# A decode stage reordered: from groups of four pages to units of one head pair, across batch boundaries

## The chip, the cores and the metric

The kernel runs on 1 core of a Trainium2 chip. The metric is the device time of one execution in microseconds (us), median of the runs. The engines are TensorE (PE, its weight loads apart as PEld), VectorE (DVE), ScalarE (ACT), GpSimd (POOL) and SyncE (SP). Each has its own instruction queue, worked off strictly in order; they meet through semaphores that the kernel waits on and raises by hand.

## The reference, cut to what matters

One inference step of a two-layer decoder trunk: a prompt of 1024 tokens and 8 decode batches of 4 new tokens each. The change touches only the decode attention of layer 0, over a paged cache of 4096 past tokens (32 pages of 128) and 8 heads of 64:

```python
kpast = cache_k[i][page_table].reshape(Bd, P, H_FOX, HEAD_DIM)
vpast = cache_v[i][page_table].reshape(Bd, P, H_FOX, HEAD_DIM)
c = jnp.cumsum(lf_all, axis=1).transpose(0, 2, 1)          # log forget values, past and new
s = jnp.einsum('bqhd,bkhd->bhqk', q, k_all) * FOX_SCALE
s = s + cq[..., :, None] - c[:, :, None, :]
p = softmax(where(kpos <= qpos, s, -inf))
o = jnp.einsum('bhqk,bkhd->bqhd', p, v_all)
```

All is float32. The kernel gets that precision by splitting an operand into a high part (fp32r) and a low part (operand minus high part), and by a matmul for each.

## The kernel before, in words

The blocks run one after the other: norm, retention, prompt attention (fox), **decode** (decode_block), output projection, and the second layer. Only decode_block changes. In it, a batch's keys come in 8 groups of 4 pages and its values in 16 pieces of 2 pages; a page of keys or values is 128 rows of 2 KB (256 KB), fetched by one DMA. What each engine does for one batch:

- SP loads keys, 4 pages a group, into a ring of 4 groups (L1555); it waits until PE has turned the group that was in that place.
- PE transposes keys (turn_keys, L1609: for each of 4 head pairs j, 4 transposes of 128x128 into PSUM bank kt[j]); computes scores (L1622, one matmul for the forget bias per group; L1626 and L1627, one each for the high and low part of each head pair); computes the scores of the new tokens (L1635, L1637); turns the probabilities (L1647, 16 transposes; L1654 for the new ones); multiplies values (L1665 and L1667, two each per piece, thus 4 matmuls a piece; at the end L1672 for the new values).
- ACT makes the high parts: of keys (L1878, one per group and head pair), of values (L1889, one per piece, 128x1024), and of scores (L1893) and probabilities (L1908). It takes the exponentials (L1899, L1901).
- DVE makes the low parts of the keys from PSUM and the high part (L1723), adds up scores (L1751) and their maxima (L1754), finds the maximum of the batch (L1760 to L1771), makes the low parts of probabilities (L1780), and writes up the heads at the end (L1803 to L1815).
- The low parts of values are divided: of pieces with p % 4 == 3 POOL makes both pages (one 128x1024 instruction); of the other 12 pieces, DVE makes the first page (L1732, 128x512) and POOL the second (L1575, 128x512).
- POOL also loads values, 4 pages a group, into a ring of 4 groups (L1566), one group late: after the two pieces of group n it waits for both low parts of group n-1 and then issues the 4 DMAs of group n+3.

High and low parts of values lie in rings of VRING = 4 pieces; a slot is free when PE has used its piece (v_used).

The order of each queue is written out by hand. There are DB + 1 rounds of 8 groups. In round r, group g, every engine does its whole part of the four head pairs of group g of batch r (PE then the scores of group g-1), and then the value pieces of batch r-1 that two tables give: SLOT_PIECES for PE (pieces 0, 1 in group 2; then three a group; 14, 15 in group 7), AHEAD_PIECES for ACT and DVE (pieces 0, 1 in group 1; 13 to 15 in group 6). The last scores of a batch, its maxima, the queries of the next batch and the heads of the batch before stand in DVE's queue between two rounds, ahead of the next round's keys (L1850 to L1856). The last round has values only.

Before the first round, PE, DVE and ACT prepare the forget biases (L1683 to L1698, L1834 to L1848); SP's loads of small tables stand ahead of them. The tile lf holds the page sums for it, and sc the scores; qz and selz are the stationary operands of the scores.

Of the kernel before, what the change touches and what calls it, by code (L numbers as in the profile page):

```python
# [18 lines left out]
F32 = mybir.dt.float32  # L19
# [1393 lines left out]
def both_on_pool(p):  # L1413

    return p % 4 == 3


def on_vector(p):

    return sum(not both_on_pool(q) for q in range(p + 1))  # L1420


def decode_block(nc, e, a):
# [18 lines left out]
    with ExitStack() as ctx:  # L1442
# [8 lines left out]
        lf = sb("lf", [P, DB, H, NPG])  # L1451
# [4 lines left out]
        qz = sb("qz", [P, pairs, ZW], F32R)  # L1456
        selz = sb("selz", [P, ZW], F32R)
# [9 lines left out]
        sc = sb("sc", [2 * rows, PAST // 2])  # L1467
# [45 lines left out]
        v_lo_first = c.begin("v_lo_first_ready", on_vector(VPIECES - 1))  # L1513
        v_lo_last = c.begin("v_lo_last_ready", VPIECES)
# [20 lines left out]
        with nc.Block() as block:  # L1535
# [24 lines left out]
            def _(pool):  # L1560
# [9 lines left out]
                def split_values(r, p):  # L1570

                    first = 0 if both_on_pool(p) else 1
                    at = VP * p % (RING * PG)
                    pool.wait_ge(v_hi_ready.sem, v_hi_ready.at(r, p + 1))
                    pool.tensor_tensor(v_lo[p % VRING][:, first:VP, :], v[:, at + first:at + VP, :],  # L1575
                                       v_hi[p % VRING][:, first:VP, :].bitcast(F32), ALU.subtract).then_inc(
                        v_lo_last.sem, 1)
# [4 lines left out]
                pool.memset(qz[:].bitcast(F32), 0.0)  # L1582
                pool.memset(selz[:].bitcast(F32), 0.0).then_inc(own_ready.sem, 1)
# [6 lines left out]
                for n in range(DB * GROUPS):  # L1590
                    r, g = n // GROUPS, n % GROUPS
                    for p in (2 * g, 2 * g + 1):
                        split_values(r, p)
                    if n > 0 and n - 1 + RING < DB * GROUPS:
                        last = n - 1
                        p = 2 * (last % GROUPS) + 1
                        pool.wait_ge(v_lo_first.sem, v_lo_first.at(last // GROUPS, on_vector(p)))
                        pool.wait_ge(v_lo_last.sem, v_lo_last.at(last // GROUPS, p + 1))
                        load_values(last + RING)

            @block.tensor
            def _(pe):
                def turn_keys(r, g):
                    landed = k_landed[g % RING]
                    pe.wait_ge(landed.sem, landed.at(r, 16 * PG * (g // RING + 1)))
                    for j in range(pairs):
                        pe.wait_ge(kt_read[j].sem, kt_read[j].at(r, g))
                        for i in range(PG):
                            ins = pe.transpose(kt[j][:, PAGE * i:PAGE * i + PAGE],  # L1609
                                               k[g % RING][:, i, P * j:P * j + P], e.ident[:])  # L1610
                        ins.then_inc(kt_written[j].sem, 1)

                def scores(r, g):
                    x, cols = g // 2, window(g)
                    bank = sbk[x % 2]
                    if g % 2 == 0:
                        pe.wait_ge(sb_read[x % 2].sem, sb_read[x % 2].at(r, x // 2))
                    if g == 0:
                        pe.wait_ge(q_ready.sem, q_ready.at(r, 1))
                    if r == 0:  # L1620
                        pe.wait_ge(ct_ready.sem, ct_ready.at(0, g + 1))
                    pe.matmul(bank[:], selz[:, cols], ct[:, BANK * g:BANK * g + BANK], start=(g % 2 == 0), stop=False)  # L1622
                    for j in range(pairs):
                        pe.wait_ge(kt_read[j].sem, kt_read[j].at(r, g + 1))
                        last = g % 2 == 1 and j == pairs - 1
                        pe.matmul(bank[:], qz[:, j, cols], k_hi[g % 2][:, j, :], start=False, stop=False)  # L1626
                        mm = pe.matmul(bank[:], qz[:, j, cols], k_lo[g % 2][:, j, :], start=False, stop=last)  # L1627
                    if g % 2 == 1:
                        mm.then_inc(sb_written[x % 2].sem, 1)
# [26 lines left out]
                def values(r, p):  # L1656
# [3 lines left out]
                    pe.wait_ge(v_lo_first.sem, v_lo_first.at(r, on_vector(p)))  # L1660
                    pe.wait_ge(v_lo_last.sem, v_lo_last.at(r, p + 1))
                    for i in range(VP):
                        n, parity = block_of(VP * p + i)
                        stationary = pt[:, n, parity, :, :].rearrange("p s c -> p (s c)")
                        pe.matmul(outb[0:2 * rows, :], stationary, v_hi[p % VRING][:, i, :],  # L1665
                                  start=(p == 0 and i == 0), stop=False)
                        mm = pe.matmul(outb[0:2 * rows, :], stationary, v_lo[p % VRING][:, i, :], start=False,  # L1667
                                       stop=False)
# [17 lines left out]
                by_page = lf[:].rearrange("p b h g -> p (b h) g")  # L1686
# [13 lines left out]
                for r in range(DB + 1):  # L1700
                    for g in range(GROUPS):
                        if r < DB:
                            turn_keys(r, g)
                            if g > 0:
                                scores(r, g - 1)
                        if r > 0:
                            if g == 1:
                                turn_probabilities(r - 1)
                            if g == 3:
                                turn_new(r - 1)  # L1710
                            for p in SLOT_PIECES.get(g, ()):
                                values(r - 1, p)
                    if r < DB:
                        new_scores(r)
                        scores(r, GROUPS - 1)

            @block.vector
            def _(dve):
                def split_keys(r, g):

                    for j in range(pairs):
                        dve.wait_ge(kt_hi[j].sem, kt_hi[j].at(r, g + 1))
                        dve.tensor_tensor(k_lo[g % 2][:, j, :], kt[j][:], k_hi[g % 2][:, j, :].bitcast(F32),  # L1723
                                          ALU.subtract).then_inc(kt_read[j].sem, 1)

                def split_values(r, p):

                    if both_on_pool(p):
                        return
                    at = VP * p % (RING * PG)  # L1730
                    dve.wait_ge(v_hi_ready.sem, v_hi_ready.at(r, p + 1))
                    dve.tensor_tensor(v_lo[p % VRING][:, 0, :], v[:, at, :], v_hi[p % VRING][:, 0, :].bitcast(F32),  # L1732
                                      ALU.subtract).then_inc(v_lo_first.sem, 1)

                def queries(r):
                    own = e.q_own[:, r, :].rearrange("p (j c) -> p j c", j=pairs)
                    hi = qz[:, :, rows:2 * rows]
                    dve.tensor_copy(hi, own).then_inc(steps_q.sem, 1)
                    dve.tensor_copy(selz[:, rows:2 * rows], pick[:, r, :])
                    dve.wait_ge(steps_q.sem, steps_q.at(r, 1))  # L1740
                    dve.tensor_tensor(qz[:, :, 3 * rows:4 * rows], own, hi.bitcast(F32), ALU.subtract).then_inc(
# [107 lines left out]
                for r in range(DB + 1):  # L1849
                    if r > 0:  # L1850
                        store_scores(r - 1, GROUPS // 2 - 1)
                        maxes(r - 1)
                        if r < DB:
                            queries(r)
                    if r > 1:
                        heads(r - 2)  # L1856
                    for g in range(GROUPS):
                        if r < DB:
                            split_keys(r, g)
                        if r > 0:  # L1860
                            if g == 1:
                                probabilities(r - 1)
                                sums(r - 1)
                            if g == 3:
                                new_probabilities(r - 1)
                            for p in AHEAD_PIECES.get(g, ()):
                                split_values(r - 1, p)
                        if r < DB and g in (2, 4, 6):
                            store_scores(r, g // 2 - 1)
                heads(DB - 1)  # L1870

            @block.scalar
            def _(act):
                def split_keys(r, g):

                    for j in range(pairs):
                        act.wait_ge(kt_written[j].sem, kt_written[j].at(r, g + 1))
                        act.activation(k_hi[g % 2][:, j, :], kt[j][:], ACT.Copy).then_inc(kt_hi[j].sem, 1)  # L1878
# [571 lines left out]
```

## Time and profile before

| what | value |
|---|---|
| median of 3 runs | 2839.48 us (2836.92 to 2842.32) |
| profiled execution, its own time | 2842.4 us |
| its span, first to last instruction | 2840.7 us |
| PE busy in the span | 2465.6 us (87%) |
| DVE, ACT, POOL busy | 1015.6, 895.5, 729.4 us |
| mean granted TensorE clock | 0.925 |
| keys and values moved in decode | 512 DMAs of 256 KB |

The profiled execution's own time is 1.7 us above its span, which lies around the span, and 2.9 us above the median. Busy shares are means over stages with different limits; decode lies from about 1068 to 1697 us of the span, and the rows below are of that stretch. "Clock" is the share of full speed (2.4 GHz) that TensorE was granted. A matmul's duration in the trace overlaps the next one's: the distance between starts is what one costs.

### The profile page before, as it was taken

How to read it: one execution, taken by the hardware profiler on the slowest of the kernel's cores; microseconds unless marked ns; L12 is line 12 of the kernel's file. 1: busy time of each engine (PE TensorE's matmuls, PEld its weight loads, DVE VectorE, ACT ScalarE, POOL GpSimd, SP SyncE). 2: the span in 40 equal slices, each digit the busy share in tenths (PEclk: the TensorE clock that was granted, in tenths of full speed). 3: DMA queues.
4: the chain of work that ended last, by engine and by line, in shares of the span. 5: the costliest groups of instructions: out<-in, count | busy, mean ns of one | idle time of the engine just before them, and what ended most of it. 6: DMA issues, size and time to landing. Idle time of an engine off the chain costs nothing. (4 is left out here: it accounts for less than half of the span.)

```text
span 2840.7 us, 36413 instructions
## 1 busy us (share of the span) xinstructions
PE 2465.6 (87%) x11784; PEld 1969.8 (69%) x11784; DVE 1015.6 (36%) x1532; ACT 895.5 (32%) x1388; POOL 729.4 (26%) x642
## 2 busy tenths in 40 slices
PE   6999999499999797777877747969988999995899
PEld 6999999377667456555555526857776888784787
DVE  3244334512443555766676650030002311131000
ACT  4232232222232223555555422141113223423200
POOL 1211111131010001555555555211112111210611
PEclk8999999699999898999899958979999999998999
DMA  5122110211200007777777525432112211212531
GB/s 131 31 51 64 41 42 24 63 45 30 52 0 23 7 16 246 253 234 235 229 241 237 175 88 166 118 135 93 63 63 95 94 62 62 91 65 82 168 95 59
DMA packets 241975, 289.12 MB, mean 102 GB/s; under 512 B 66954, under 2 KB 169740, under 8 KB 241740
## 3 DMA queue, kind: packets, MB, share of 16 engines
q1 hardware_dynamic: 203548, 185.00, 22.3%
q0 software_dynamic: 20480, 67.13, 6.9%
q10 hardware_dynamic: 17840, 35.69, 3.5%
q8 instruction: 52, 0.85, 0.1%
q14 instruction: 55, 0.45, 0.0%
HBM read 247.47 MB, written 41.32 MB: 102 GB/s over the span
## 5 line engine op out<-in xcount | busy, mean ns | idle before, releaser
L201 PE MATMUL bank<-whi,x_hi 128*128 128x512 f32 (+1 forms) x1728 | 663.6, 384 | 33.1 <-POOL wlo L188 27.4
L205 PE MATMUL bank<-whi,x_lo 128*128 128x512 f32 (+1 forms) x1728 | 655.7, 379 | 0.0
L203 PE MATMUL bank<-wlo,x_hi 128*128 128x512 f32 (+1 forms) x1728 | 654.8, 379 | 0.0
L188 POOL TENSOR_TENSOR wlo<-wraw,whi 128x512 fp32r<-128x512 f32 (+1 forms) x192 | 227.2, 1218 | 853.5 <-ACT whi L181 853.5
L201 PEld LDWEIGHTS bank<-whi,x_hi 128*128 128x128 f32 x1728 | 328.4, 190 | 100.8 <-POOL wlo L188 24.8
L230 ACT ACTIVATE projected<-bank 128x512 f32<-128x512 f32 (+1 forms) x216 | 120.4, 563 | 798.1 <-PE bank L205 777.4
L205 PEld LDWEIGHTS bank<-whi,x_lo 128*128 128x128 f32 x1728 | 328.7, 190 | 52.3
L203 PEld LDWEIGHTS bank<-wlo,x_hi 128*128 128x128 f32 x1728 | 329.7, 191 | 50.1 <-issue 0.4
L1575 POOL TENSOR_TENSOR dec_v_lo<-dec_v,dec_v_hi 128x512 fp32r<-128x512 f32 (+1 forms) x128 | 205.6, 1625 | 230.5 <-ACT dec_v_hi L1889 229.6
L1665 PE MATMUL bank<-dec_v_hi,dec_pt 128*64 128x512 f32 x256 | 111.8, 437 | 89.7 <-POOL dec_v_lo L1575 55.6
L1609 PE MATMUL bank<-ident,dec_k 128*128 128x128 f32 x1024 | 154.7, 315 | 40.3 <-DVE dec_kt_lo L1723 38.4
L1609 PEld LDWEIGHTS bank<-ident,dec_k 128*128 128x128 f32 x1024 | 143.8, 166 | 54.3 <-issue 43.1
L1732 DVE TENSOR_TENSOR dec_v_lo<-dec_v,dec_v_hi 128x512 fp32r<-128x512 f32 x96 | 154.9, 1640 | 58.9 <-ACT dec_v_hi L1889 58.3
L1878 ACT ACTIVATE dec_kt_hi<-bank 128x512 fp32r<-128x512 f32 x256 | 138.0, 602 | 118.7 <-PE bank L1609 117.8
L1723 DVE TENSOR_TENSOR dec_kt_lo<-bank,dec_kt_hi 128x512 fp32r<-128x512 f32 x256 | 163.2, 681 | 33.3 <-ACT dec_kt_hi L1878 32.2
L501 PE MATMUL bank<-out_whi,out_mhi 128*128 128x512 f32 x392 | 154.7, 395 | 12.0 <-POOL out_mlo L482 12.0
L2224 DVE SCALAR_TENSOR_TENSOR gm_m<-bank,gm_bias,gm_ug 128x256 f32<-128x256 f32 x64 | 25.8, 476 | 359.1 <-ACT gm_ug L2252 359.1
L502 PE MATMUL bank<-out_wlo,out_mhi 128*128 128x512 f32 x392 | 154.0, 393 | 0.0
L503 PE MATMUL bank<-out_whi,out_mlo 128*128 128x512 f32 x392 | 153.9, 393 | 0.0
L534 DVE TENSOR_TENSOR out_y<-bank,out_x 128x512 f32<-128x512 f32 (+1 forms) x36 | 24.5, 689 | 346.5 <-PE bank L503 263.9
L1566 POOL DMA_DIRECT2D dec_v<-cache_v x256 | 137.8, 541 | 39.5 <-issue 36.8
L1889 ACT ACTIVATE dec_v_hi<-dec_v 128x1024 fp32r<-128x1024 f32 x128 | 128.7, 1053 | 36.9 <-PE bank L1667 25.6
(279 smaller groups left out, 3396.8 us busy)
## 6 DMA issues: line engine op xcount, KB each, us to landing
dec_v<-cache_v POOLq DMA_DIRECT2D x256, 256.0 KB, 4.0
dec_k<-cache_k SPq DMA_DIRECT2D x256, 256.0 KB, 3.1
wraw<-w_in_even SPq DMA_DIRECT2D x32, 512.0 KB, 5.9
wraw<-w_in_odd SPq DMA_DIRECT2D x16, 1024.0 KB, 8.3
gv<-projected ACTq DMA_DIRECT2D x4, 2304.0 KB, 8.3
gm_v<-gv SPq DMA_DIRECT2D x8, 1152.0 KB, 5.9
m<-gm_mt ACTq DMA_DIRECT2D x8, 1056.0 KB, 4.1
wraw<-w_in_odd SPq DMA_DIRECT2D x4, 2048.0 KB, 8.8
```

The source lines that it names most:

```text
L188: pool.tensor_tensor(e.wlo[:, k, 0:width], e.wraw[:, k, 0:width], e.whi[:, k, 0:width].bitcast(F32), ALU.subtract).then_inc(e.w_ready.sem, 1)
L201: pe.matmul(bank[:, 0:width], e.xhi[:, k, c:c + P], e.whi[:, k, 0:width], start=(k == 0), stop=False)
L203: pe.matmul(bank[:, 0:width], e.xhi[:, k, c:c + P], e.wlo[:, k, 0:width], start=False, stop=False)
L205: mm = pe.matmul(bank[:, 0:width], e.xlo[:, k, c:c + P], e.whi[:, k, 0:width], start=False, stop=(k == KD - 1))
L501: pe.matmul(bank[:], mhi[slot][:, k, :], whi[:, k, cols], start=(k == 0), stop=False)
L502: pe.matmul(bank[:], mhi[slot][:, k, :], wlo[:, k, cols], start=False, stop=False)
L503: mm = pe.matmul(bank[:], mlo[slot][:, k, :], whi[:, k, cols], start=False, stop=(k == kt - 1))
L1575: pool.tensor_tensor(v_lo[p % VRING][:, first:VP, :], v[:, at + first:at + VP, :], v_hi[p % VRING][:, first:VP, :].bitcast(F32), ALU.subtr ...
L1609: ins = pe.transpose(kt[j][:, PAGE * i:PAGE * i + PAGE], k[g % RING][:, i, P * j:P * j + P], e.ident[:])
L1723: dve.tensor_tensor(k_lo[g % 2][:, j, :], kt[j][:], k_hi[g % 2][:, j, :].bitcast(F32), ALU.subtract).then_inc(kt_read[j].sem, 1)
L1732: dve.tensor_tensor(v_lo[p % VRING][:, 0, :], v[:, at, :], v_hi[p % VRING][:, 0, :].bitcast(F32), ALU.subtract).then_inc(v_lo_first.sem, 1)
L1878: act.activation(k_hi[g % 2][:, j, :], kt[j][:], ACT.Copy).then_inc(kt_hi[j].sem, 1)
```

## The change

Decode's order is rewritten in units u of one head pair: 32 units a batch (4 head pairs times 8 groups), running through from batch to batch without a break. In unit u, PE turns the keys of head pair u % 4 of group u / 4 and computes the scores of the same head pair of the group before; ACT and DVE split that head pair. The other work is hung in at fixed units after a batch's first: the sums of scores at 12, 20, 28 and 36 (the last with the maxima), new scores and the next batch's queries at 20, exponentials at 38, probabilities at 42, new probabilities and sums at 43, value piece p on PE at 44 + 3p/2 (thus 44 to 66), on ACT five units earlier and on DVE four units earlier, heads at 68. So batch r's values run beside batch r+1's keys from its unit 12 to its unit 34, that is up to 2 units into batch r+2.

Also:
- The low part of a value piece is made whole, in one 128x1024 instruction: on DVE for p % 3 == 2 (5 of 16 pieces), on POOL for the other 11.
- POOL issues the loads of group n+4 right after the second piece of group n (no longer one group late), and waits ahead of them for DVE's low part where one of the two pieces is DVE's.
- VRING goes from 4 to 5; qz and selz get two buffers each (two more memsets on POOL ahead of the first load); lf and sc share one tile.

The core of the diff (the semaphores and declarations that only follow from it are left out):

```diff
-VRING = 4
+VRING = 5
-SLOT_PIECES = {2: (0, 1), 3: (2, 3, 4), 4: (5, 6, 7), 5: (8, 9, 10), 6: (11, 12, 13), 7: (14, 15)}
-AHEAD_PIECES = {1: (0, 1), 2: (2, 3), 3: (4, 5, 6), 4: (7, 8, 9), 5: (10, 11, 12), 6: (13, 14, 15)}
+SLOTS = H // 2
+UNITS = GROUPS * SLOTS
+NEW_AT, EXP_AT, TURN, FIRST_VALUE, LEAD = 20, UNITS + 6, UNITS + 10, UNITS + 12, 5
+LOW = [2 * SLOTS * x + 3 * SLOTS for x in range(GROUPS // 2)]
+VALUE_AT = [FIRST_VALUE + 3 * p // 2 for p in range(VPIECES)]
+HEADS_AT = VALUE_AT[-1] + 2
 def on_vector(p):
-    return sum(not both_on_pool(q) for q in range(p + 1))
+    return p % 3 == 2
+def rounds_at(u, at):
+    r = (u - at) // UNITS
+    return r if (u - at) % UNITS == 0 and 0 <= r < DB else None
+def pieces_at(u, lead):
+    return [(r, p) for r in range(DB) for p in range(VPIECES) if UNITS * r + VALUE_AT[p] - lead == u]
...
 # POOL
+                for i in range(2):
+                    pool.memset(qz[i][:].bitcast(F32), 0.0)
+                    ins = pool.memset(selz[i][:].bitcast(F32), 0.0)
+                ins.then_inc(own_ready.sem, 1)
...
+                for n in range(DB * VPIECES):
+                    r, p = n // VPIECES, n % VPIECES
+                    if not on_vector(p):
                         split_values(r, p)
+                    following = n // 2 + RING
+                    if p % 2 == 1 and following < DB * GROUPS:
+                        if on_vector(p) or on_vector(p - 1):
+                            pool.wait_ge(v_lo_vector.sem, v_lo_vector.at(r, by_vector(p)))
+                        if not on_vector(p) or not on_vector(p - 1):
+                            pool.wait_ge(v_lo_pool.sem, v_lo_pool.at(r, by_pool(p)))
+                        load_values(following)
...
 # PE
+                for u in range(UNITS * (DB - 1) + HEADS_AT):
+                    n, j = u // SLOTS, u % SLOTS
+                    if n < DB * GROUPS:
+                        turn_keys(n // GROUPS, n % GROUPS, j)
+                    if 0 < n <= DB * GROUPS:
+                        scores((n - 1) // GROUPS, (n - 1) % GROUPS, j)
+                    if rounds_at(u, NEW_AT) is not None:
+                        new_scores(rounds_at(u, NEW_AT))
+                    if rounds_at(u, TURN) is not None:
+                        turn_probabilities(rounds_at(u, TURN))
+                    if rounds_at(u, TURN + 1) is not None:
+                        turn_new(rounds_at(u, TURN + 1))
+                    for r, p in pieces_at(u, 0):
+                        values(r, p)
...
 # DVE
+                for u in range(UNITS * (DB - 1) + HEADS_AT + 3):
+                    n, j = u // SLOTS, u % SLOTS
+                    for x in range(GROUPS // 2):
+                        r = rounds_at(u, LOW[x])
+                        if r is not None:
+                            store_scores(r, x)
+                            if x == GROUPS // 2 - 1:
+                                maxes(r)
+                    if n < DB * GROUPS:
+                        split_keys(n // GROUPS, n % GROUPS, j)
+                    if rounds_at(u, NEW_AT) is not None and rounds_at(u, NEW_AT) + 1 < DB:
+                        queries(rounds_at(u, NEW_AT) + 1)
+                    if rounds_at(u, TURN) is not None:
+                        probabilities(rounds_at(u, TURN))
+                    if rounds_at(u, TURN + 1) is not None:
+                        new_probabilities(rounds_at(u, TURN + 1))
+                        sums(rounds_at(u, TURN + 1))
+                    for r, p in pieces_at(u, LEAD - 1):
+                        if on_vector(p):
+                            split_values(r, p)
+                    if rounds_at(u, HEADS_AT) is not None:
+                        heads(rounds_at(u, HEADS_AT))
...
 # ACT
+                for u in range(UNITS * (DB - 1) + HEADS_AT + 3):
+                    n, j = u // SLOTS, u % SLOTS
+                    for x in range(GROUPS // 2):
+                        if rounds_at(u, LOW[x]) is not None:
+                            low_scores(rounds_at(u, LOW[x]), x)
+                    if n < DB * GROUPS:
+                        split_keys(n // GROUPS, n % GROUPS, j)
+                    if rounds_at(u, EXP_AT) is not None:
+                        exponentials(rounds_at(u, EXP_AT))
+                    if rounds_at(u, TURN) is not None:
+                        probabilities(rounds_at(u, TURN))
+                    for r, p in pieces_at(u, LEAD):
+                        split_values(r, p)
```

## Rows read from the trace of the kernel before

**Rows 1.** Stretches: us; PE, PEld, DVE, ACT, POOL busy (count); clock; DMA share, GB/s.
```profile
1099.00:1132.30 33.30, 33.30 (x211) 29.11 (x212) 25.13 (x40) 19.24 (x36) 0.00 (x0) 0.95 0.66 192
1132.30:1635.50 503.20, 389.67 (x2052) 288.78 (x2050) 348.39 (x521) 271.49 (x421) 294.49 (x332) 0.91 0.70 228
1635.50:1690.00 54.50, 31.77 (x83) 14.05 (x83) 34.84 (x31) 20.34 (x24) 36.67 (x36) 0.59 0.29 97
```
**Rows 2.** Last step of a batch's maximum: ns min/median/max, first and last start.
```profile
L1771 DVE TENSOR_SCALAR dec_neg_max<-dec_top x8: 144/144/144, 1135.4 to 1635.5; 32x1 f32<-32x1 f32 x8
```
**Rows 3.** PE in order of time, batches 0 and 1: start, us, instruction, count.
```profile
1104.27 0.48 PE L1622 MATMUL bank<-dec_ct,dec_selz 128*128 128x512 f32 x1
...
1129.51 0.44 PE L1635 MATMUL bank<-k_new,q_own 128*32 128x32 f32 x8
...
1130.05 0.50 PE L1622 MATMUL bank<-dec_ct,dec_selz 128*128 128x512 f32 x1
...
1142.18 1.20 PE L1647 MATMUL bank<-ident,dec_sc 64*128 64x64 f32 x16
```
**Rows 4.** PE in order of time, the value matmuls of two pieces (eight).
```profile
1309.11 0.39 PE L1665 MATMUL bank<-dec_v_hi,dec_pt 128*64 128x512 f32 x1
...
1310.72 0.40 PE L1667 MATMUL bank<-dec_v_lo,dec_pt 128*64 128x512 f32 x1
```
**Rows 5.** Waits in 1099 to 1690 us: who, for whom; total us, times, longest.
```profile
PE bank L1665 <- POOL dec_v_lo L1575: 55.6, 39, 2.3
...
PE bank L1609 <- DVE dec_kt_lo L1723: 38.4, 7, 5.9
PE bank L1665 <- DVE dec_v_lo L1732: 33.9, 21, 4.1
...
POOL dec_v L1566 <- issue: 26.2, 43, 2.0
```
**Rows 6.** PE in order of time, one boundary between batches.
```profile
1425.34 3.65 PE L1609 MATMUL bank<-ident,dec_k 128*128 128x128 f32 x16 [5.94 <-DVE dec_kt_lo L1723]
```
**Rows 7.** Groups by line and shape, 900 to 1760 us: busy us, mean ns, idle.
```profile
L1723 DVE TENSOR_TENSOR dec_kt_lo<-bank,dec_kt_hi 128x512 fp32r<-128x512 f32 x256 | 163.2, 681 | 33.3 <-ACT dec_kt_hi L1878 32.2
L1732 DVE TENSOR_TENSOR dec_v_lo<-dec_v,dec_v_hi 128x512 fp32r<-128x512 f32 x96 | 154.9, 1640 | 58.9 <-ACT dec_v_hi L1889 58.3
...
L1566 POOL DMA_DIRECT2D dec_v<-cache_v x256 | 137.8, 541 | 39.5 <-issue 36.8 <-PE bank L1683 0.6
L1575 POOL TENSOR_TENSOR dec_v_lo<-dec_v,dec_v_hi 128x512 fp32r<-128x512 f32 x96 | 130.6, 1372 | 194.2 <-ACT dec_v_hi L1889 193.4
L1889 ACT ACTIVATE dec_v_hi<-dec_v 128x1024 fp32r<-128x1024 f32 x128 | 128.7, 1053 | 36.9 <-PE bank L1667 25.6 <-DMA dec_v<-cache_v 11.3
...
L1575 POOL TENSOR_TENSOR dec_v_lo<-dec_v,dec_v_hi 128x1024 fp32r<-128x1024 f32 x32 | 76.3, 2384 | 36.2 <-ACT dec_v_hi L1889 36.2
```
**Rows 8.** All engines in order of time around one DVE low part of values.
```profile
1365.23 4.47 DVE L1732 TENSOR_TENSOR dec_v_lo<-dec_v,dec_v_hi 128x512 fp32r<-128x512 f32 x1
...
1365.52 3.62 POOL L1575 TENSOR_TENSOR dec_v_lo<-dec_v,dec_v_hi 128x512 fp32r<-128x512 f32 x2
```
**Rows 9.** DVE's low parts of values: ns min/median/max.
```profile
L1732 DVE TENSOR_TENSOR dec_v_lo<-dec_v,dec_v_hi x96: 668/1423/6641, 1145.4 to 1679.6; 128x512 fp32r<-128x512 f32 x96
```
**Rows 10.** Stretches (columns as in rows 1): before the first batch, and within a round.
```profile
1080.00:1096.00 16.00, 14.66 (x114) 13.83 (x113) 7.08 (x12) 3.21 (x6) 4.29 (x8) 0.79 1.02 399
1440.00:1460.00 20.00, 15.15 (x74) 10.24 (x73) 15.50 (x20) 10.36 (x16) 16.88 (x20) 0.93 0.89 304
```
**Rows 11.** All engines in order of time ahead of the first batch.
```profile
1068.39 0.62 POOL L1582 MEMSET dec_qz<- 128x640 f32 x1
...
1074.83 0.30 PEld L1683 LDWEIGHTS bank<-ident,dec_v 128*128 128x128 f32 x2 [12.80 <-DMA dec_own_head<-c_own_head]
```
**Rows 12.** POOL and DVE in order of time, end of decode.
```profile
1669.06 10.04 POOL L1575 TENSOR_TENSOR dec_v_lo<-dec_v,dec_v_hi 128x512 fp32r<-128x512 f32 x6
...
1689.51 0.24 DVE L1815 TENSOR_SCALAR dec_o<-dec_o_hi,dec_inv_sum 32x64 f32<-32x64 f32 x1
```

More of the change, by code:

```diff
@@ L1455, in decode_block @@
         ct = sb("ct", [P, PAST], F32R)
-        qz = sb("qz", [P, pairs, ZW], F32R)
-        selz = sb("selz", [P, ZW], F32R)
+        qz = [sb(f"qz{i}", [P, pairs, ZW], F32R) for i in range(2)]
+        selz = [sb(f"selz{i}", [P, ZW], F32R) for i in range(2)]
         k = [sb(f"k{i}", [P, PG, WF]) for i in range(RING)]
@@ L1601, in _, with turn_keys @@
             @block.tensor
             def _(pe):
-                def turn_keys(r, g):
+                def turn_keys(r, g, j):
                     landed = k_landed[g % RING]
[L1605 to L1611, printed above, removed]
@@ L1623, in scores @@
[L1623 to L1628, printed above, removed]
+                    if j == 0:
+                        if g % 2 == 0:
+                            pe.wait_ge(sb_read[x % 2].sem, sb_read[x % 2].at(r, x // 2))
+                        if g == 0:
+                            pe.wait_ge(q_ready.sem, q_ready.at(r, 1))
+                        if r == 0:
+                            pe.wait_ge(ct_ready.sem, ct_ready.at(0, g + 1))
+                        pe.matmul(bank[:], selz[r % 2][:, cols], ct[:, BANK * g:BANK * g + BANK], start=(g % 2 == 0),
+                                  stop=False)
@@ L1629, in scores @@
+                    pe.wait_ge(kt_read[j].sem, kt_read[j].at(r, g + 1))
+                    last = g % 2 == 1 and j == pairs - 1
+                    pe.matmul(bank[:], qz[r % 2][:, j, cols], k_hi[g % 2][:, j, :], start=False, stop=False)
+                    mm = pe.matmul(bank[:], qz[r % 2][:, j, cols], k_lo[g % 2][:, j, :], start=False, stop=last)
+                    if last:
                         mm.then_inc(sb_written[x % 2].sem, 1)
@@ L1717, in _, with split_keys @@
             @block.vector
             def _(dve):
[L1719 to L1724, printed above, removed]
+                def split_keys(r, g, j):
+                    dve.wait_ge(kt_hi[j].sem, kt_hi[j].at(r, g + 1))
+                    dve.tensor_tensor(k_lo[g % 2][:, j, :], kt[j][:], k_hi[g % 2][:, j, :].bitcast(F32),
+                                      ALU.subtract).then_inc(kt_read[j].sem, 1)
@@ L1848, in _ @@
                                           ALU.subtract).then_inc(ct_ready.sem, 1)
[L1849 to L1869, printed above, removed]
@@ L1872, in _, with split_keys @@
             @block.scalar
             def _(act):
[L1874 to L1878, printed above, removed]
+                def split_keys(r, g, j):
+                    act.wait_ge(kt_written[j].sem, kt_written[j].at(r, g + 1))
+                    act.activation(k_hi[g % 2][:, j, :], kt[j][:], ACT.Copy).then_inc(kt_hi[j].sem, 1)
@@ L1919, in _ @@
                         ct_hi.sem, 1)
[L1920 to L1937 removed]
+                for u in range(UNITS * (DB - 1) + HEADS_AT + 3):
[11 more added lines that the diff above has]
+                        split_values(r, p)
+                    if rounds_at(u, HEADS_AT + 2) is not None:
+                        store(rounds_at(u, HEADS_AT + 2))
                 act.wait_ge(out_stored.sem, out_stored.at(DB, 0))
```

121 lines of the change are left out of this document (38 added, 83 removed).

## The prediction

> **What bounds the kernel now.** I read the page first, for where decode lies, then the table of stretches. Decode's steady part is 503.2 us in which PE is busy for 389.67, DVE for 348.39, ACT for 271.49 and POOL for 294.49, at clock 0.91 [rows 1]. No engine is full, so the loss is in how they wait for one another. The maxima give the period: eight of them from 1135.4 to 1635.5, thus 500.1 / 7 = 71.4 us a batch [rows 2]. Ahead lies the first batch (33.3 us, PE busy throughout), behind it a tail of 54.5 us with values only, PE busy for 31.77 at clock 0.59 [rows 1].
>
> What would PE need? In batch 0 only keys and scores run. From the first bias matmul (1104.27) to the last (1130.05) lie seven groups of scores, six of transposes and one set of new scores (0.54) [rows 3]. A wide matmul costs 0.23 us from start to start (1.61 / 7, rows 4 stand for it) [rows 4], so nine of a group's scores cost 2.1, seven such groups 14.6, and six groups of transposes the remaining 10.7, 1.8 each. A batch of keys and scores is 8 x 3.9 = 31 us. Values are 64 matmuls x 0.23 = 14.7; turning probabilities is 1.2 [rows 3], new scores 0.5, new values and their turn some 1. PE's floor is **48.5 us a batch** against 71.4.
>
> The 23 us between show in the waits: PE stood 55.6 + 33.9 us before L1665 for low parts of values and 38.4 us for key banks, the latter in 7 waits of up to 5.9 us [rows 5]. Seven is the number of boundaries between batches: there DVE and ACT first finish the old batch's scores, maxima and heads, and PE, with all four banks turned, stands; one stood 5.94 [rows 6]. The half speed after such a stop adds to it (clock 0.91 in the steady part, 0.95 in batch 0) [rows 1].
>
> **The change part by part.** The profiled execution took 2842.4 us, 2.9 above the median; I subtract what is saved from the median.
>
> *Units and the boundary.* PE can stay four head pairs ahead at any time, and the sums of a batch's last scores stand at unit 36, behind PE's unit 35 and ahead of nothing that PE needs within three units. I take the 38.4 / 7 = 5.5 us a batch as gone. No instruction is added by it; 2 x 0.23 of scores now follow each four transposes. DVE's heads (about 3 us) and sums come between key splits in smaller bits; their cover is the slack of four units, 3.9 us without values and 6.4 with them. A head block of 3 us thus costs nothing beside values and could cost 1 where it stands, at unit 68, after the values' end.
>
> *Value pieces.* On PE a piece falls every 1.5 units. A unit is 3.9 / 4 = 0.97 us without values, 1.58 with them (plus 2/3 x 0.92). ACT begins at unit 39 and PE ends at 66: 27 units, 26.2 + 14.7 + 2.0 (probabilities and the new tokens) = 43 us of PE. The other 5 units are 5.7 us.
>
> *POOL.* It must fit its part into those 27 units, for ring slots come free only as PE uses pieces. A whole piece took 2.38, its loads 0.54 each [rows 7]: 11 x 2.33 (2.38 less the overlap of one instruction with the next) = 25.6; seven groups of loads x 4 x 0.54 = 15.1; gaps in the loads, 26.2 us in eight batches [rows 5], 3. The new waits ahead of loads: pieces 5 and 11 are DVE's and directly precede a load, so POOL stands for one low part each, 2 x 1.35 (twice the 0.67 of half a piece [rows 9]) = 2.7. The waits behind pieces 3, 9 and 15 concern the piece before, which DVE can make during the preceding loads; I give 1.5 for the collisions. With 1.05 for ACT's first high part [rows 7] the sum is 49. So POOL's queue and not PE's would set the window: 49 + 5.7 = 54.7. Today the same window is looser, since 12 pieces are divided.
>
> *DVE.* Busy 348.39 in 7.04 periods, 49.5 a batch [rows 1], of it 154.9 / 8 = 19.4 for low parts of values [rows 7]; 30 remain. Half a piece takes 0.67 undisturbed, but 1.64 on average and 6.64 at worst [rows 7, 9]. One took 4.47 while POOL ran two low parts (3.62 together), and ended 0.56 after them [rows 8]: it got no turn between them. The Trainium skill (SBUF — State Buffer, "SBUF: two separate sides") says a DVE instruction with two SBUF inputs and a GpSimd one share a port as an exclusive lock, held for the whole instruction. The trace agrees that one blocks the other, but not that the wait ends with one instruction: by that rule the 4.47 would have been nearer 2, and each of the new waits at most one piece, 2.4 us. I go by the row. Five whole pieces with 2 us of waiting each are 5 x 3.35 = 17, so DVE comes to 47: not the bound, but with little slack, and keys queue behind each wait. The bounds of what surfaces of these 10 us at PE are 0 and 10; rows 8 and the four units of cover are nearest to little, I take 2.3. **Period: 57 us.**
>
> *ACT.* 271.49 / 7.04 = 38.6 us a batch [rows 1], unchanged: below every bound. SP only loads keys, and earlier by a fraction of a group.
>
> *Transfers.* A batch is 64 pages of 256 KB, 16.8 MB: 235 GB/s at 71.4 us, 294 at 57. The busiest 20 us of a round moved 304 GB/s, and 399 GB/s ran where little else did [rows 10]: 55 us at the first, 42 at the second. They are covered, barely by the first. The Trainium skill (HBM Reference, opening table) gives about 358 GB/s per core; the 399 here is above it, and 358 would mean 47 us, not a bound either.
>
> *Ahead of the first batch.* The extra memsets are 0.62 + 0.22 [rows 11], and PE waits 12.8 us there for a table's transfer until 1074.83 [rows 11]; POOL is done by 1070. Nothing, as long as that transfer lasts. Batch 0 stays 33 us.
>
> *The tail.* The last exponentials must still precede the last values, but ACT may now split pieces 0 and 1 before the probabilities: POOL starts some 2 us sooner. Then it has 11 x 2.33 and four groups of loads, 34 us, near today's 36.67 busy [rows 1]. At the end POOL ran low parts for 10.04 us without a break [rows 12], and DVE's pieces 11 and 14 can be shut out by such a run. I take 4 us saved, between 0 and 8. Work after 1689.75 [rows 12] does not change.
>
> The sum: 7 x (71.4 - 57) = 101, plus 4, is 105 us. 2839.5 - 105 = **2735 us**.
>
> **The rivals.** *A: PE is the bound.* POOL's waits vanish in the idle five units and the period is 50. For it: PE was busy without a gap in batch 0 with the same chain. Against it: POOL's 49 us in 43. It saves 7 x 21.4 + 4 = 154: 2685 us.
>
> *B: DVE is the bound.* Each of its five pieces waits out a pair of POOL's, 4.7 us. That is 30 + 5 x (1.35 + 4.7) = 60 with 3 us of dependence at each end: period 63, and nothing saved in the tail: 2839.5 - 59 = 2780 us. For it: rows 8; against it: pairs are always followed by loads.
>
> *C: slower.* POOL's queue now stops ahead of a load until DVE has made its piece, and DVE stops until POOL is out: each stands for the other in turn. POOL's work, 25.6 + 17.3 + 3 + 1.5 = 47, plus five stops of the longest row (6.64 [rows 9]) is 80.6 us a batch: 2839.5 + 7 x 9.2 = 2904 us. It decides from stops of (71.4 - 47) / 5 = 4.9 us each. Against it: the mean today is 1.
>
> *D: no gain.* The transfers don't come faster than the 228 GB/s of today [rows 1]; then the period stays, and 2836 us comes out. Against it rows 10. That the order written is not the order run is in this case too (a wait in a wrong place that chains the batches again).
>
> **How the numbers follow.** Forecast (period 54 to 60) 0.52; A 0.23; B and between it and the forecast 0.17; C 0.05; D 0.03. The range takes in A down to PE's floor of 48.5 us (7 x 22.9 + 4 = 164, thus 2675) and B (2780); of A, B and the forecast it leaves out little, of C and D all. Below 0.2% (5.7 us), about what a measurement of this kernel can tell from no change, is only D, in part: same 0.02, slower 0.05, faster 0.93.
>
> **What would show it.** Right: maxima 57 us apart; no wait of PE on key banks over 2 us; POOL busy over 75% in the steady part, and PE's largest wait on POOL's low parts; clock above 0.95 there; over 280 GB/s. A shows PE busy over 95% and POOL waiting for ACT; B shows DVE's low parts above 5 us each and PE waiting for L1723's successor; C shows POOL waiting for DVE ahead of loads by tens of us a batch. A period under 50 or over 64, or a tail changed by more than 8 us, makes the working wrong.

## The result and the profile after

The changed kernel takes 2894.47 us (median of 4, 2893.12 to 2898.11), the kernel before beside it 2839.05: the ratio is 1.0194, 95% interval 1.0178 to 1.021. I had forecast 2735 and a range up to 2780: wrong in sign and outside the range. The profiled execution has a span of 2891.8 us, 51.1 above that of before.

The maximum's last step and the stretches, as in [rows 1, 2], of the kernel after (columns: us; PE, PEld, DVE, ACT, POOL busy; clock; DMA share; GB/s):

```profile
L1792 DVE TENSOR_SCALAR dec_neg_max<-dec_top x8: 144/144/145, 1138.4 to 1681.8; 32x1 f32<-32x1 f32 x8
```

```profile
1138.40:1681.80 543.40, 409.30 (x2015) 279.31 (x2013) 302.38 (x459) 270.33 (x413) 304.90 (x301) 0.86 0.66 211
1681.80:1740.00 58.20, 29.35 (x83) 13.56 (x83) 20.27 (x21) 20.24 (x24) 34.39 (x27) 0.64 0.25 73
```

The period is (1681.8 - 1138.4) / 7 = 77.6 us in place of 71.4; the tail to the last write-up of heads is 59.3 us (1681.8 to 1741.1) in place of 54.0, and the first maximum comes 3.0 later, of which 1.7 lie ahead of decode (below). 7 x 6.2 + 5.3 + 3.0 = 51.7 accounts for the difference of the spans. Every engine is emptier than before: PE is busy for 409.30 of 543.4 us (75%, where it was 77%), POOL for 56% in place of 59%; the clock fell to 0.86, transfers to 211 GB/s.

The table of waits of the kernel after, of its decode:

```profile
...
POOL dec_v L1587 <- issue: 183.7, 234, 3.1
PEld bank L1691 <- POOL dec_v_lo L1595: 163.3, 66, 6.9
PE bank L1691 <- POOL dec_v_lo L1595: 132.6, 56, 6.0
POOL dec_v_lo L1595 <- ACT dec_v_hi L1908: 111.2, 8, 51.9
...
ACT dec_v_hi L1908 <- PE bank L1693: 26.5, 10, 7.0
...
PE bank L1631 <- DVE dec_kt_lo L1746: 13.7, 9, 2.4
...
POOL dec_v L1587 <- DVE dec_v_lo L1753: 7.9, 6, 1.6
...
PE bank L1691 <- DVE dec_v_lo L1753: 2.3, 1, 2.3
```

Two things went the way that was forecast: PE's waits for key banks fell from 38.4 us to 13.7, and its waits for DVE's low parts from 33.9 to 2.3. But waits for POOL's rose from 55.6 to 132.6, and third in the whole table, behind two waits of ACT and DVE for each other's keys, stands a line that was further down in [rows 5]: POOL idle ahead of its loads of values, released by "issue", that is by nothing in the trace's semaphores: 183.7 us where it was 26.2. The waits that the profile puts down to DVE are another 7.9 us.

POOL in order of time after the change, one low part, one group of loads, the next low part:

```profile
1420.83 2.36 POOL L1595 TENSOR_TENSOR dec_v_lo<-dec_v,dec_v_hi 128x1024 fp32r<-128x1024 f32 x1
1424.46 0.56 POOL L1587 DMA_DIRECT2D dec_v<-cache_v  x1 [1.27 <-issue]
1425.61 0.54 POOL L1587 DMA_DIRECT2D dec_v<-cache_v  x1 [0.59 <-issue]
1426.75 0.54 POOL L1587 DMA_DIRECT2D dec_v<-cache_v  x1 [0.60 <-issue]
1427.89 0.54 POOL L1587 DMA_DIRECT2D dec_v<-cache_v  x1 [0.61 <-issue]
1428.45 2.38 POOL L1595 TENSOR_TENSOR dec_v_lo<-dec_v,dec_v_hi 128x1024 fp32r<-128x1024 f32 x1
```

The low part ends at 1423.19; its successor starts at 1428.45, 5.3 us later, for four loads that are busy for 0.54 each. The first stands 1.27 us off, the others 0.6. What POOL does in the gaps shows in the line that reads page numbers, for those 5 us. POOLq is POOL's sequencer (min/median/max ns, first and last start):

```profile
L1585 POOLq TENSOR_LOAD <-dec_page_table x4: 288/290/295, 1423.3 to 1426.7; - x4
L1585 POOLq FUSED_REGOPS  x4: 152/152/152, 1423.6 to 1427.0; - x4
```

Each load needs its page number from the table in SBUF (0.29 us), then register work (0.15 and more). The four reads lie from 1423.3 to 1426.7, one per load, 1.15 apart, and begin only when the low part has ended. In the trace, 60 groups of loads from 1100 us on stand this way, with 3.0 to 3.4 us of gaps each (5.6 in two).

### The profile page after: what moved, and what is told of

It is laid out like the page before. It is cut to its first block and busy times, and to the rows that moved or that the text cites. A ratio compares the mean times of both kernels' runs of the same rounds, so it can differ in the third digit from the quotient of the medians.

```text
span 2891.8 us, 36167 instructions
## 1 busy us (share of the span) xinstructions
PE 2487.8 (86%) x11784; PEld 1964.2 (68%) x11784; DVE 963.8 (33%) x1476; ACT 902.2 (31%) x1388; POOL 738.5 (26%) x604
## 3 DMA queue, kind: packets, MB, share of 16 engines
q1 hardware_dynamic: 203548, 185.00, 21.6%
## 5 line engine op out<-in xcount | busy, mean ns | idle before, releaser
L1746 DVE TENSOR_TENSOR dec_kt_lo<-bank,dec_kt_hi 128x512 fp32r<-128x512 f32 x256 | 170.6, 685 | 223.4 <-ACT dec_kt_hi L1898 222.8
L1691 PE MATMUL bank<-dec_v_hi,dec_pt 128*64 128x512 f32 x256 | 122.8, 480 | 135.6 <-POOL dec_v_lo L1595 132.6
L1595 POOL TENSOR_TENSOR dec_v_lo<-dec_v,dec_v_hi 128x1024 fp32r<-128x1024 f32 x88 | 209.1, 2390 | 112.0 <-ACT dec_v_hi L1908 111.2
L1898 ACT ACTIVATE dec_kt_hi<-bank 128x512 fp32r<-128x512 f32 x256 | 151.0, 597 | 264.4 <-PE bank L1631 256.5
L1587 POOL DMA_DIRECT2D dec_v<-cache_v x256 | 139.0, 543 | 202.1 <-issue 193.5
L1631 PE MATMUL bank<-ident,dec_k 128*128 128x128 f32 x1024 | 172.3, 296 | 15.5 <-DVE dec_kt_lo L1746 13.7
L1691 PEld LDWEIGHTS bank<-dec_v_hi,dec_pt 128*64 128x64 f32 x256 | 40.6, 158 | 187.7 <-POOL dec_v_lo L1595 163.3
L1908 ACT ACTIVATE dec_v_hi<-dec_v 128x1024 fp32r<-128x1024 f32 x128 | 134.6, 1054 | 27.7 <-PE bank L1693 26.5
```

Source lines behind the costliest of these rows:

```text
L1595: pool.tensor_tensor(v_lo[slot][:], v[:, at:at + VP, :], v_hi[slot][:].bitcast(F32), ALU.subtract).then_inc(v_lo_pool.sem, 1)
L1631: ins = pe.transpose(kt[j][:, PAGE * i:PAGE * i + PAGE], k[g % RING][:, i, P * j:P * j + P], e.ident[:])
L1691: pe.matmul(outb[0:2 * rows, :], stationary, v_hi[slot][:, i, :], start=(p == 0 and i == 0), stop=False)
```

## The experiments

Theory S: the new position of the loads makes POOL wait for the low part that it has just started. The wait is satisfied by its own engine, but the sequencer stops at it, and the page numbers, which it used to read while the low part ran, are read afterwards with the engine idle. Rival C is the prediction's: DVE and POOL stop each other over whole pieces. Rival U: units of one head pair are slow in themselves.

**lag**: the change with the loads one group late, as before it.

```diff
-                    following = n // 2 + RING
-                    if p % 2 == 1 and following < DB * GROUPS:
-                        if on_vector(p) or on_vector(p - 1):
-                            pool.wait_ge(v_lo_vector.sem, v_lo_vector.at(r, by_vector(p)))
-                        if not on_vector(p) or not on_vector(p - 1):
-                            pool.wait_ge(v_lo_pool.sem, v_lo_pool.at(r, by_pool(p)))
-                        load_values(following)
+                    last = n // 2 - 1
+                    if p % 2 == 1 and last >= 0 and last + RING < DB * GROUPS:
+                        lr, lp = last // GROUPS, 2 * (last % GROUPS) + 1
+                        pool.wait_ge(v_lo_vector.sem, v_lo_vector.at(lr, by_vector(lp)))
+                        pool.wait_ge(v_lo_pool.sem, v_lo_pool.at(lr, by_pool(lp)))
+                        load_values(last + RING)
```

> The changed kernel, with POOL's loads of values issued one group late again (after the pieces of group n those of group n+3, waiting for the low parts of group n-1), all else as changed. Theory S (POOL's sequencer waits for the piece that it has just started, so the page number of each load is read only after it: 1.14 us a load in place of 0.54, and 1.2 us more ahead of the first): the idle time ahead of loads falls from 193 to under 40 us, the period of a batch from 77.6 to 55-60 us, the time to about 2750 (2730-2780). Rival C (DVE and POOL stop each other over whole pieces): the waits stay, the time stays above 2860. Rival U (units of one head pair are themselves slower, through the short chain PE, ACT, DVE per bank): not under 2840.

Measured: 2730.26 us, ratio 0.961 (0.9581 to 0.9638). Rows of this run: maxima, the steady stretch, POOL's idle time ahead of loads, and POOL in order of time with the reads of its sequencer:

```profile
L1791 DVE TENSOR_SCALAR dec_neg_max<-dec_top x8: 144/144/144, 1136.5 to 1528.2; 32x1 f32<-32x1 f32 x8
```

```profile
1136.50:1528.20 391.70, 355.82 (x2015) 254.89 (x2012) 305.84 (x458) 271.12 (x413) 300.26 (x297) 0.97 0.84 290
```

```profile
its engine sat idle before it (us, times) until:
  issue: 17.4, 34
```

The reads of page numbers around the low part of 1431.14, on POOL's sequencer:

```profile
L1585 POOLq TENSOR_LOAD <-dec_page_table x4: 286/288/293, 1430.6 to 1434.0; - x4
```

POOL itself at that place:

```profile
1431.14 2.42 POOL L1595 TENSOR_TENSOR dec_v_lo<-dec_v,dec_v_hi 128x1024 fp32r<-128x1024 f32 x1
1433.48 2.26 POOL L1587 DMA_DIRECT2D dec_v<-cache_v  x4
1435.76 2.39 POOL L1595 TENSOR_TENSOR dec_v_lo<-dec_v,dec_v_hi 128x1024 fp32r<-128x1024 f32 x1
```

The idle time ahead of loads is 17.4 us (after: 193.5 over the whole run), four loads take 2.26 us in one piece, and the period is 391.7 / 7 = 56.0. The reads still stand 1.15 apart, but three of the four begin before the low part ends at 1433.56, and only the last, at 1434.0, beside the loads. Rivals C and U both fall with the time: the one wanted above 2860, the other not under 2840. PE is busy for 91% of the stretch, at clock 0.97. What PE still waits for there (1130 to 1515 us):

```profile
PE bank L1630 <- DVE dec_kt_lo L1745: 19.5, 16, 2.5
...
PE bank L1690 <- POOL dec_v_lo L1595: 2.3, 2, 1.3
```

**before_nolag**: the same position of the loads, in the old order.

```diff
-                    if n > 0 and n - 1 + RING < DB * GROUPS:
-                        last = n - 1
+                    if n + RING < DB * GROUPS:
+                        last = n
```

> The kernel before, with its loads of values issued right after the group's own pieces (group n+4 after group n, waiting for the low parts of group n), order of groups as before. Theory S: the loads cost up to 8 x 2.4 + 8 x 0.7 us of POOL more a batch, some of it in POOL's idle time: 2880-2980. Rival C: only the short wait for DVE's half pieces is added, under 2 us a batch: 2840-2860. Rival U: no change, 2839.

Measured: 2971.53 us, ratio 1.0462 (1.0434 to 1.049), period 88.4. POOL's idle time ahead of loads is 177.6 us to "issue" and 30.6 to DVE. So the position, with its waits, costs 17.0 us a batch in the old order and 21.6 in the new; and the new order gains 15.4 with late loads, 10.8 with early ones. Each part of the change keeps its sign beside the other, and they add up to within 4.6 us a batch.

**lag_own_wait**: a single wait put back into lag; the loads stay late.

```diff
-                        pool.wait_ge(v_lo_pool.sem, v_lo_pool.at(lr, by_pool(lp)))
+                        pool.wait_ge(v_lo_pool.sem, v_lo_pool.at(r, by_pool(p)))
```

> The kernel with the loads one group late, with one wait changed: ahead of a group's loads POOL waits for the low part that it has itself just started, not for the one of a group ago. The loads stay late. Theory S in its narrow form (the wait for its own latest instruction is what lets the reading of page numbers out into the open): back to the changed kernel's time less DVE's share, 2870-2900, with 160-200 us idle ahead of loads. If it is the lag itself, or the wait for DVE, that matters: 2730.

Measured: 2895.93 us, ratio 1.0192 (1.0168 to 1.0215), the changed kernel's own. This run's waits:

```profile
POOL dec_v L1587 <- issue: 172.4, 224, 3.1
...
PE bank L1690 <- POOL dec_v_lo L1595: 138.0, 56, 7.2
```

One wait, for something that costs the engine nothing to wait for, makes the whole difference: in the trace each group of loads has 3.1 to 3.4 us of gaps again (5.6 in two), without the changed kernel's wait for DVE. What the delay then holds up is not the same engine by engine: ACT waits 74.3 us for value pages here, for the loads are late as well.

**pages_first**: the changed kernel; the four numbers of a group are read ahead of the two waits, which are kept.

```diff
+                        pages = page_numbers(following)
                         if on_vector(p) or on_vector(p - 1):
...
-                        load_values(following)
+                        load_values(following, pages)
```

> The changed kernel, where POOL reads the four page numbers of a group ahead of the waits and issues the four loads after them; what is waited for is the same. Theory S: the 0.60 us between two loads goes and part of the 1.2 ahead of the first, some 2.4 us a group, 15-19 a batch: 2765-2810. Rivals C and U: the waits are the same and so is the time, 2885-2895.

Measured: 2769.86 us, ratio 0.9747 (0.9721 to 0.9774), period 60.5. POOL in this run:

```profile
1404.21 4.74 POOL L1598 TENSOR_TENSOR dec_v_lo<-dec_v,dec_v_hi 128x1024 fp32r<-128x1024 f32 x2
1409.59 2.29 POOL L1590 DMA_DIRECT2D dec_v<-cache_v  x4 [0.65 <-POOL dec_v_lo L1598]
1411.90 2.40 POOL L1598 TENSOR_TENSOR dec_v_lo<-dec_v,dec_v_hi 128x1024 fp32r<-128x1024 f32 x1
```

The gaps between loads are gone; 0.65 us ahead of the first stay, since the wait does: 40.0 us in 58 such gaps, some 5 a batch, near the 4.5 that this kernel's period is above lag's. So it is the reading, behind the wait, that cost most.

**read_twice**, the changed kernel, and **lag_read_twice**, lag, with a second reading of each page number ahead of the one used:

```diff
+                        pool.value_load(table[0:1, r * NPG + PG * g + j:r * NPG + PG * g + j + 1], min_val=0,
+                                        max_val=n_phys - 1)
```

> The changed kernel, where POOL reads each page number twice (0.29 + 0.15 us of its sequencer more per load). Theory S: 32 x 0.46 = 15 us a batch on the path: 2970-3005. Rivals C and U: POOL's sequencer is not the bound, 2890-2905.

> The kernel with the loads one group late, each page number read twice. The same 0.46 us a load cost the changed kernel 124 us. Theory S: POOL's low parts (2.4 to 4.7 us a group) cover 4 x (0.6 + 0.46) us in most groups: under a third of that, 2730-2770. If reading costs wherever it stands: 2830-2860.

Measured: 3018.78 us, ratio 1.0627 (1.0594 to 1.0661), period 93.7, 16.1 more than without: the whole price, and 14 us above my range, for a second reading adds 0.53 us to each load (1.13 between two loads in place of 0.60) and not 0.46. And 2806.12 us, ratio 0.9882 (0.9858 to 0.9905), period 65.6, 9.6 more: more than I expected, and between my two ranges. The reason stands in POOL's order of lag_read_twice:

```profile
1410.75 2.42 POOL L1597 TENSOR_TENSOR dec_v_lo<-dec_v,dec_v_hi 128x1024 fp32r<-128x1024 f32 x1
1413.11 1.12 POOL L1589 DMA_DIRECT2D dec_v<-cache_v  x2
1415.36 0.54 POOL L1589 DMA_DIRECT2D dec_v<-cache_v  x1 [1.13 <-issue]
1417.04 0.54 POOL L1589 DMA_DIRECT2D dec_v<-cache_v  x1 [1.14 <-issue]
```

Two of four loads are covered by the low part, two stand in the open, 1.68 us apart. The sequencer needs 1.14 us a load, 4.6 a group, and the engine 2.15 for the loads and 11 x 2.33 / 8 = 3.2 for low parts, 5.4: read once, the sequencer keeps up by a little; read twice it needs 4 x 1.68 = 6.7 and is the slower of the two. The difference (8 x 1.3 = 10) is near the measured 9.6.

**half_lag**: lag, but issued after the first piece of the next group.

```diff
-                    if p % 2 == 1 and last >= 0 and last + RING < DB * GROUPS:
+                    if p % 2 == 0 and last >= 0 and last + RING < DB * GROUPS:
```

> The changed kernel, with POOL's loads of group n+4 issued after the first piece of group n+1: a lag of one piece and not of a group. Theory S: what counts is that one POOL instruction runs while the sequencer reads; in front of a load there is one whole piece of 2.4 us at most (none where the first piece of a group is DVE's), so much of the 2.4 us of reading is covered: between the lag of a group and none, 2735-2800. Without theory S: 2885-2895.

Measured: 2837.22 us, ratio 0.9981 (0.9969 to 0.9994), period 70.5: outside what I expected. In the trace, three groups in eight have 3.1 us of gaps or more ahead of and between their loads, as after the change: those where the first piece of the next group is DVE's, so that POOL runs nothing between the wait and the loads. In the other five one low part of 2.4 us hides nearly all of it: 0.2 to 0.8 us stay in most. Together that is some 12 us a batch, of the 14.5 that the period is above lag's.

**lag_pages**: lag and pages_first together.

```diff
+                        pages = page_numbers(last + RING)
...
-                        load_values(last + RING)
+                        load_values(last + RING, pages)
```

> The kernel with the loads one group late, and in it the four page numbers read ahead of the wait and the loads. Theory S: 17 us of such gaps are left in all, not all on the path: 2715-2732. If the gaps between loads have another cause than the reading: no change, 2730.

Measured: 2738.03 us, ratio 0.9627 (0.961 to 0.9643), lag's own within the intervals, and outside my range for theory S (2715 to 2732). Next to nothing was left to hide: of lag's 17.4 us only 7.0 lie behind 1100 us, and in lag_pages 3.9 of such gaps and 5.2 of waits for low parts stand there. So this run tells nothing for or against the reading; pages_first does.

**values_sp**: the value loads in SP's queue, sorted in by unit; none on POOL.

```diff
+                todo = [(SLOTS * (n - RING) + SLOTS - 1, 0, n) for n in range(RING, DB * GROUPS)]
+                todo += [(UNITS * ((n - RING) // GROUPS) + VALUE_AT[2 * ((n - RING) % GROUPS) + 1] - 1, 1, n)
+                         for n in range(RING, DB * GROUPS)]
+                for _, values_, n in sorted(todo):
+                    (load_values if values_ else load_keys)(n)
```

> The changed kernel, with the loads of values in SP's queue, in the order of the units, and none on POOL. POOL loses 17 us of work a batch and its reading. Theory S, if the cost of a page is one of any queue: SP's loads stood 1.1 us apart ahead of the first batch, and 64 a batch make 70 us: the period is 70 and the time 2830-2850, with SP as the bound. If instead POOL's work alone was the bound: period 49-52 of PE, 2680-2705.

Measured: 2819.07 us, ratio 0.9919 (0.9902 to 0.9936), period 69.1: 11 us below my range, but near the period of 70. SP becomes the bound with 64 loads a batch at 1.1 us: from 1140 to 1620 us it waits for others 1.2 us in all, and others wait for its loads:

```profile
ACT dec_v_hi L1908 <- DMA dec_v<-cache_v: 113.2, 28, 7.8
...
PE bank L1631 <- DMA dec_k<-cache_k: 25.3, 9, 4.1
```

**lag_vector_wait**: lag, with the changed kernel's wait for DVE's low part ahead of the loads.

```diff
-                        pool.wait_ge(v_lo_vector.sem, v_lo_vector.at(lr, by_vector(lp)))
+                        if on_vector(p) or on_vector(p - 1):
+                            pool.wait_ge(v_lo_vector.sem, v_lo_vector.at(r, by_vector(p)))
+                        else:
+                            pool.wait_ge(v_lo_vector.sem, v_lo_vector.at(lr, by_vector(lp)))
```

> The kernel with the loads one group late, but where one of a group's pieces is DVE's, POOL waits for that low part before the (late) loads, as the changed kernel does. Rival C (POOL and DVE stop each other): 2800 and more. Theory S: where DVE has finished before POOL the wait costs nothing, and where it has not (pieces 5 and 11) POOL stands and also reads in the open, 2 of 8 groups: 5 us a batch at most, 2730-2765.

Measured: 2779.77 us, ratio 0.9788 (0.9772 to 0.9804), period 62.6: 6.6 us a batch, between both expectations. The profile gives POOL's idle time ahead of loads to "issue" (61.1 us in 68 gaps) and none to DVE, but the order of time separates the two. POOL, then DVE, then the read by POOL's sequencer:

```profile
1425.97 2.39 POOL L1595 TENSOR_TENSOR dec_v_lo<-dec_v,dec_v_hi 128x1024 fp32r<-128x1024 f32 x1
1430.95 0.56 POOL L1587 DMA_DIRECT2D dec_v<-cache_v  x1 [2.59 <-issue]
```

```profile
1428.53 1.21 DVE L1755 TENSOR_TENSOR dec_v_lo<-dec_v,dec_v_hi 128x1024 fp32r<-128x1024 f32 x1
```

```profile
L1585 POOLq TENSOR_LOAD <-dec_page_table x1: 293/293/293, 1429.8 to 1429.8; - x1
```

POOL is done at 1428.36, DVE at 1429.74, and the read follows at once: 1.4 us of the 2.59 are DVE's lateness, the rest is reading in the open. So it is in two groups in eight, as theory S said, for the first six batches (4.1 to 4.7 us of gaps each, 6.7 in one), and the other groups have hardly any. Over all, 15.1 us of the 61.1 are DVE's lateness. My bound of 5 us a batch was too low: the two groups make about 8.8 of gaps a batch, and the period grew by 6.6.

**lag_halves**: lag, with the old division (12 pieces halved, 4 whole on POOL).

```diff
-    return p % 3 == 2
+    return p % 4 != 3
...
-                    pool.tensor_tensor(v_lo[slot][:], v[:, at:at + VP, :], v_hi[slot][:].bitcast(F32),
+                    first = 1 if on_vector(p) else 0
+                    pool.tensor_tensor(v_lo[slot][:, first:VP, :], v[:, at + first:at + VP, :],
```

> The kernel with the loads one group late, and the low parts of values divided as before (12 pieces in halves between DVE and POOL, 4 whole on POOL). If whole pieces make DVE and POOL stop each other (rival C): 2700-2720. If they save waits (5 stops of DVE a batch in place of 12): slower, 2740-2770.

Measured: 2738.74 us, ratio 0.963 (0.9614 to 0.9646): the same as lag, within the intervals, and in neither of my ranges. With late loads whole pieces neither cost nor gain, which speaks against rival C and against my own opposite expectation.

**lag_spread**: lag with a value piece every 1.75 units.

```diff
-VALUE_AT = [FIRST_VALUE + 3 * p // 2 for p in range(VPIECES)]
+VALUE_AT = [FIRST_VALUE + 7 * p // 4 for p in range(VPIECES)]
```

> The kernel with the loads one group late, with a value piece every 1.75 units in place of 1.5 (units 44 to 70, heads at 72), so that POOL's and PE's value work fills 31 of 32 units. If POOL's 43 us in 27 units still hold PE up: 2700-2720. If PE's 91% busy is all there is to have: 2725-2740.

Measured: 2709.58 us, ratio 0.9536 (0.9519 to 0.9552), the fastest kernel of the study. The period is 53.7; in the stretch from 1136 to 1510 us PE is busy for 352.06 of 374, 94%. Its waits from 1130 to 1515 us stand below:

```profile
1136.00:1510.00 374.00, 352.06 (x2014) 258.38 (x2013) 284.36 (x456) 271.25 (x414) 297.72 (x291) 0.95 0.88 299
```

```profile
PE bank L1676 <- DVE dec_pt L1800: 20.3, 7, 3.1
PE bank L1690 <- POOL dec_v_lo L1595: 2.7, 2, 1.9
...
PE bank L1630 <- DVE dec_kt_lo L1745: 0.3, 1, 0.3
```

The time is the one expected, the reason is not. POOL held PE up for 2.3 us in lag's steady stretch and for 2.7 here, so nothing was to be had there. What went are PE's waits for key banks (19.5 to 0.3) and DVE's low parts (6.1 to 0.5), while those for probabilities rose (3.7 to 20.3). Which of the shifted works does it was not tried.

## Why the prediction was wrong

**The step that failed** is the term for POOL: "seven groups of loads x 4 x 0.54 + gaps in the loads, 3". I took 0.54 from the engine's row [rows 7] and the gaps from the waits of before [rows 5]. Both are right for a queue whose sequencer is ahead. A group of loads really costs 5.3 us behind a wait for the low part just started, not 2.15 + 0.4: 2.7 us more, seven times within the window, 19 us. 57 + 19 = 76, against 77.6 measured. Measured from lag, it is all eight groups that count: 8 x 2.7 = 21.6, and 77.6 - 56.0 = 21.6. The diff showed both new waits. I gave a price only to the one for DVE's low part (7.9 us in all as measured); the one for POOL's own, just started, has no term in the sum. It costs the engine nothing, but its sequencer everything that it did meanwhile.

**The rest of the sum** comes near in lag, which is the change without that one position: period 56.0 against 57, tail 49.0 (1528.2 to 1577.2) against 50, time 2730 against 2735. That is in part luck. My 57 held 2.7 + 1.5 for the waits for DVE's low parts, and lag has none of these; without them my terms give 52.8, and with them lag_vector_wait took 62.6. And I had POOL's queue set the window, while in lag PE waits for POOL's low parts 2.3 us in the whole steady stretch and for key banks 19.5. These waits I took as gone, 5.5 us a batch. The stop at a boundary fell from 5.95 us to 2.4 at most after the change and to 2.5 in lag; it did not go.

**The tail** grew by 5.3 where I gave 4 of gain: POOL has four groups of loads there, exposed in the same way: 4 x 2.7 = 10.8, and lag's tail is 10.3 shorter.

**Ahead of the first batch**, the two memsets were set at nothing. The first maximum is 3.0 us later after the change and 1.1 in lag, but decode's first memset starts at 1068.19 before, 1069.90 after and 1067.72 in lag: from there on it is 1.3 and 1.6 us more. It was not tried which part is the memsets'.

**Rival C** came out nearest (2904) for a wrong reason. Its place was right, the waits ahead of POOL's loads, but its price was to be DVE's stops, and POOL's waits for DVE were 7.9 us in decode, not 5 x 6.64 a batch. lag_own_wait takes it away, for it has the changed kernel's time without the new wait for DVE. Rival D fell: lag moved 290 GB/s in its steady stretch. Rival A, PE as the bound, is what lag_spread comes near to (PE 94% busy, period 53.7 where A had 50). My use of the Trainium skill (HBM Reference, "Specifications (TRN2)") was partial: the text under the table gives about 425 GB/s for a core that streams alone, and 358 as the share with its neighbour busy too. The 399 GB/s of [rows 10] lies between the two, nearer the first.

## What to carry to other kernels

An engine's queue, as POOL's and SP's show here, has two rates, that of its units and that of its sequencer, and before a wait is moved one should count what the sequencer does behind it (reads of indices, registers, issues) and which long instruction covers that. A wait for the engine's own latest instruction looks free in every table of busy times and empties the run-ahead; wait for an older one, or read what is needed ahead of the wait. When a profile's idle time is released by "issue", look at the sequencer's lines in that stretch first.

## What the runs showed of the hardware

POOL's sequencer takes 1.14 us for a load with a page number read from SBUF, whether the engine is idle (after: reads 1.15 apart in the open) or not (lag: 1.15 apart behind a low part). Of it 0.66 go to the read (0.29), the register work (0.15) and small steps, and the rest to issuing the load: in pages_first, where the numbers are read beforehand, four loads take 2.29, thus 0.57 each. It read three page numbers before a low part of 2.42 us had ended, and in lag all four loads then start back to back. The Trainium skill (DMA: Bandwidth & Descriptors, "Latency and other measured facts") gives about 600 ns as the floor of a `tensor_load` and does not say what that covers. The read itself took 0.29 here, below it; what a first reading adds to a load is 0.60 and a second 0.53, so the page's figure fits the whole of a reading and not the instruction.

Busy time of DVE's low parts says little: in the changed kernel a whole piece took 1.22 us in the median and 7.24 at the worst, while PE waited for it 2.3 us in all.
